# Query and key projections of an attention stage as 512- and 256-column products into two PSUM banks each

## The reference

```python
for i in range(DEPTH):
    x = x + 0.5 * swiglu(rmsnorm(x, ln_gains[i, 0]), w_gate[i, 0], w_up[i, 0], w_down[i, 0])
    h = rmsnorm(x, ln_gains[i, 1])
    x = x + (moba_attention(h, w_qkv, w_o) if i % 2 == 0 else pool_mixer(h, pool_w, pool_scale))
    x = x + 0.5 * swiglu(rmsnorm(x, ln_gains[i, 2]), w_gate[i, 1], w_up[i, 1], w_down[i, 1])
return rmsnorm(x, final_gain)
```

## Time and profile before

| | us |
|---|---|
| median of 3 runs | 876.4 (876.39 to 876.97) |
| profiled execution | 878.0, of which the span from first to last instruction is 876.0 |
| TensorE busy | 866.6 |
| VectorE busy | 642.9 |
| ScalarE busy | 463.2 |
| weight loads on TensorE (beside its products) | 763.4 |

### The profile page before, as it was taken

One profiled execution on the slowest core, in us unless ns is written; L12 is line 12 of the kernel. 1 busy time (PEld: TensorE's weight loads), 2 busy tenths in 40 slices (PEclk: granted clock), 3 DMA queues, 4 the chain that ended last, 5 costly groups with the idle time before them and its releaser, 6 DMA issues.

```text
span 876.0 us, 12479 instructions
## 1 busy us (share of the span) xinstructions
PE 866.6 (99%) x5234; PEld 763.4 (87%) x5234; DVE 642.9 (73%) x742; ACT 463.2 (53%) x536; POOL 22.7 (3%) x49
## 2 busy tenths in 40 slices
PE   8999999999999999999999999999999999999997
PEld 7888888889999988888888888888888988888886
DVE  6998776568776699777656697777656998777452
ACT  6665555345555666555534375555544675555441
POOL 1000005300000000000000000000000000000000
PEclk9999999999999999999999999999999999999999
DMA  8677555565434447555455556555565277565431
GB/s 285 197 249 231 191 176 174 181 201 180 149 144 146 144 137 247 193 191 182 164 196 187 185 187 200 191 192 181 170 196 175 97 241 234 184 213 186 146 119 48
DMA packets 154166, 159.68 MB, mean 182 GB/s; under 512 B 2888, under 2 KB 152448, under 8 KB 154112
## 3 DMA queue, kind: packets, MB, share of 16 engines
q1 hardware_dynamic: 153760, 158.35, 55.5%
q10 hardware_dynamic: 352, 0.55, 0.2%
HBM read 157.84 MB, written 1.05 MB: 181 GB/s over the span
## 4 chain that ended last, share of the span: by engine, by line
PE 98%; DMA 1%; DVE 0%; SPq 0%; ACT 0%; issue 0%; DVEq 0%; ACTq 0%
PE psum L430 97%; DMA band<-in_x_dram 1%; PE psum L744 1%; PE psum L727 1%; PE psum L460 0%; PE psum L618 0%; ACT soft L917 0%; SPq L366 0%; SPq L364 0%; DVE band L1184 0%; DVE scratch L1227 0%; DVE scratch L1196 0%; DVEq L75 0%; DVE mean L1208 0%; DVE rstd L1091 0%
## 5 line engine op out<-in xcount | busy, mean ns | idle before, releaser
L430 PE MATMUL psum<-xg,w_hi 128*128 128x512 f32 (+1 forms) x1664 | 490.1, 379 | 0.1
L1046 DVE TENSOR_TENSOR w_lo<-raw,w_hi 128x2048 fp32r<-128x2048 f32 (+1 forms) x149 | 332.3, 2232 | 109.8 <-ACT w_hi L825 109.8
L430 PEld LDWEIGHTS psum<-xg,w_lo 128*128 128x128 f32 x1536 | 289.0, 188 | 62.5
L825 ACT ACTIVATE w_hi<-raw 128x2048 fp32r<-128x2048 f32 (+1 forms) x150 | 279.5, 1867 | 112.5 <-PE psum L430 112.0
L430 PE MATMUL psum<-xg,w_lo 128*128 128x256 f32 x1536 | 312.8, 278 | 0.0
L430 PEld LDWEIGHTS psum<-xg,w_hi 128*128 128x128 f32 x1664 | 254.4, 189 | 1.8 <-issue 0.9
L430 PE MATMUL psum<-h_all,w_hi 128*128 128x512 f32 (+1 forms) x656 | 189.4, 374 | 0.0
L430 PEld LDWEIGHTS psum<-h_all,w_lo 128*128 128x128 f32 x592 | 111.4, 188 | 23.4
L430 PE MATMUL psum<-h_all,w_lo 128*128 128x256 f32 x592 | 121.8, 278 | 0.0
L430 PEld LDWEIGHTS psum<-h_all,w_hi 128*128 128x128 f32 x656 | 100.2, 189 | 0.8 <-issue 0.8
L859 ACT ACTIVATE scratch<-psum 128x512 f32<-128x512 f32 x44 | 26.1, 594 | 80.8 <-PE psum L430 80.8
(11 more groups left out here) (114 smaller groups left out, 477.5 us busy)
## 6 DMA issues: line engine op xcount, KB each, us to landing
raw<-in_ffn_w_up_dram SPq DMA_DIRECT2D x43, 1024.0 KB, 5.1
raw<-in_ffn_w_gate_dram SPq DMA_DIRECT2D x42, 1024.0 KB, 5.1
raw<-in_ffn_w_down_dram SPq DMA_DIRECT2D x24, 1024.0 KB, 5.2
raw<-in_attn_w_qkv_dram SPq DMA_DIRECT2D x12, 1024.0 KB, 5.2
raw<-in_ffn_w_down_dram SPq DMA_DIRECT2D x20, 512.0 KB, 4.4
raw<-in_ffn_w_down_dram SPq DMA_DIRECT2D x12, 768.0 KB, 4.4
raw<-in_attn_w_o_dram SPq DMA_DIRECT2D x4, 1024.0 KB, 4.9
band<-in_x_dram SPq DMA_DIRECT2D x4, 256.0 KB, 5.2
```

The source lines that it names most:

```text
L430: return nc.tensor.matmul(out, stationary, moving, start=start, stop=stop, skip_group_check=True)
L825: nc.scalar.activation(w_hi[:, n % SPL, 0:size], raw[:, n % RAW, 0:size], ACT.Copy).then_inc(hi_split, 1)
L1046: nc.vector.tensor_tensor(w_lo[:, n % SPL, 0:size], raw[:, n % RAW, 0:size], w_hi[:, n % SPL, 0:size].bitcast(f32), ALU.subtract).then_inc ...
```

## The change

Q and K tiles use `split_products`: per chunk and column half one 512-column product and one 256-column product. Each column half m has a bank of its own, so Q takes banks 0 and 1, K banks 2 and 3, and V moves to bank 0. The scores of quads 0 to 2 move to banks 4 to 7, the output of quads 0 to 2 to bank 3. ScalarE copies the correction halves of Q and K into `q_sb` and `k_sb` (`copy_corrections`); VectorE adds the main halves, waits for that addition, and scales in place.

The waits on TensorE change with the banks. The Q tile of quad j waits for `qkv_scaled >= 3 * j`, the V scaling of the quad before, where it waited for the Q scaling of that quad. The K tile of quads 2 and 3 waits for the output of quad j - 2. The V tile waits for the Q scaling of its own quad, and did not wait at all for quad 0. `values(j, 0)` waits for the K scaling of quad j + 1. The first output tile waits for `o_lo` of quad 0 alone. The orders in which VectorE and ScalarE call their steps stay as they were, with `copy_corrections` put in.

```diff
         def head_bank(quad, hh):
-            return (3, 4, 5, 6)[hh] if quad < QUADS - 1 else (3, 1, 0, 2)[hh]
+            return (4, 5, 6, 7)[hh] if quad < QUADS - 1 else (1, 2, 0, 3)[hh]
         def o_bank(quad):
-            return (7, 7, 0, 3)[quad]
+            return 3 if quad < QUADS - 1 else 1
+        def qk_acc(s):
+            return psum[:, 2 * s:2 * s + 2, :]
...
-                    for m in range(GM):
-                        cols = slice(m * P, (m + 1) * P)
-                        last = passes(acc_bank(b)[:, m, :], hi[:, k, cols], lo[:, k, cols], xg_hi[:, k, :],
-                                      xg_lo[:, k, :], start=(k == 0 and m == 0), stop=(k == DC - 1))
+                    last = split_products([(banks[m], hi[:, k, m * P:(m + 1) * P], lo[:, k, m * P:(m + 1) * P],
+                                            xg[:, k], k == 0, k == DC - 1) for m in range(GM)])
...
-                if j:
-                    pe.wait_ge(qkv_scaled, 3 * (j - 1) + s + 1)
-                elif s == 0:
-                    pe.wait_ge(x_done, DC + 6)
+                if s == 0:
+                    if j:
+                        pe.wait_ge(qkv_scaled, 3 * j)
+                    else:
+                        pe.wait_ge(x_done, DC + 6)
+                elif s == 1:
+                    if j > 1:
+                        pe.wait_ge(o_lo_done, j - 1)
+                else:
+                    pe.wait_ge(qkv_scaled, 3 * j + 1)
                 if s < 2:
-                    column_product(n, s, norm, stats_norm)
+                    column_product(n, (2 * s, 2 * s + 1), norm, stats_norm)
                     return
...
-                        out = psum[:, 2, t * GW:(t + 1) * GW]
+                        out = psum[:, 0, t * GW:(t + 1) * GW]
...
-                pe.wait_ge(o_lo_done, max(j + 1, 2))
+                pe.wait_ge(o_lo_done, j + 1)
...
-                    if j == QUADS - 2:
-                        pe.wait_ge(qkv_scaled, 3 * (QUADS - 1) + 1)
+                    if j < QUADS - 1:
+                        pe.wait_ge(qkv_scaled, 3 * (j + 1) + 2)
...
+            def copy_corrections(j, s):
+                act.wait_ge(tile_used, ATT0 + 3 * j + s + 1)
+                nc.scalar.activation((q_sb, k_sb)[s][:, j % 2], qk_acc(s)[:, :, SEQ:2 * SEQ],
+                                     ACT.Copy).then_inc(qk_corr, 1)
+            copy_corrections(0, 0)
+            copy_corrections(0, 1)
             split_hi(ATT0 + SPL)
             split_hi(ATT0 + 1 + SPL)
...
-                    split_hi(ATT0 + 3 * j + 2 + SPL)
-                    split_hi(ATT0 + 3 * j + 3 + SPL)
+                    for s in range(2):
+                        split_hi(ATT0 + 3 * j + 2 + s + SPL)
+                        copy_corrections(j + 1, s)
...
             def qkv_scale(j, s):
-                dve.wait_ge(tile_used, ATT0 + 3 * j + s + 1)
+                if s < 2:
+                    done = 2 * j + s + 1
+                    qk = (q_sb, k_sb)[s][:, j % 2]
+                    dve.wait_ge(qk_corr, done)
+                    nc.vector.tensor_tensor(qk, qk_acc(s)[:, :, 0:SEQ], qk, ALU.add).then_inc(qk_sum, 1)
+                    dve.wait_ge(qk_sum, done)
                 if s == 0:
-                    ins = nc.vector.scalar_tensor_tensor(out=q_sb[:, j % 2], in0=acc_bank(0), scalar=HD ** -0.5,
-                                                         in1=rstd_m, op0=ALU.mult, op1=ALU.mult)
+                    ins = nc.vector.scalar_tensor_tensor(out=qk, in0=qk, scalar=HD ** -0.5, in1=rstd_m,
+                                                         op0=ALU.mult, op1=ALU.mult)
                 elif s == 1:
-                    ins = nc.vector.tensor_tensor(k_sb[:, j % 2], acc_bank(1), rstd_m, ALU.mult)
-                else:
+                    ins = nc.vector.tensor_tensor(qk, qk, rstd_m, ALU.mult)
+                else:
+                    dve.wait_ge(tile_used, ATT0 + 3 * j + s + 1)
                     for t in range(TT):
-                        ins = nc.vector.tensor_scalar(v_sb[:, j % 2, t, :], psum[:, 2, t * GW:(t + 1) * GW],
+                        ins = nc.vector.tensor_scalar(v_sb[:, j % 2, t, :], psum[:, 0, t * GW:(t + 1) * GW],
```

More of the change, by code:

```diff
@@ L208, in build_trunk @@
         qkv_scaled = sem("qkv_scaled")
+        qk_corr = sem("qk_corr")
+        qk_sum = sem("qk_sum")
         score_done = sem("score_done")
@@ L639, in _, with column_product @@
             ffn(0)
-            def column_product(n, b, norm=None, stats_norm=None):
+            def column_product(n, banks, norm=None, stats_norm=None):
                 hi, lo = col_tile(w_hi, n), col_tile(w_lo, n)
```

## The result

The changed kernel takes 890.3 us (median of 5, 887.8 to 891.6) against 877.0 us before: a ratio of 1.0148 (1.0137 to 1.0158), 13.4 us slower. A second set of runs gave 889.3 and 877.1, ratio 1.0132 (1.0119 to 1.0146), 12.2 us slower. The forecast was 887.3, 10.9 us slower, in a range of 885.5 to 890.5; of the 3.0 us between forecast and median 0.6 lies in the base, which was 876.4 when the forecast was made. The measured median is 0.2 us inside the upper end of the range.

A forecast was written before the change was run, and what follows sets the result against it. TensorE, busy 99% of the span, was taken as the bound, so every new wait adds in full. -1.48 (products) + 2.87 and 7.95 (stalls) + 1.6 (clock) = +10.9 us on 876.4: 887.3 us, range 885.5 to 890.5.

The forecast's parts named there:

- Part 1: Query and key tiles: one 512- and one 256-column product a group gain 0.185 us a tile, 1.48 us in all.
- Part 2: Correction copies on ScalarE (4.8 us) and additions on VectorE (some 5.7 us) cost nothing while under TensorE's stream.
- Part 3: V of quad 0, now sharing bank 0, must wait for Q's scaling: TensorE stalls 2.9 us.
- the short stall: TensorE's wait ahead of V of quad 0 for Q of quad 0 to be scaled, put at 2.9 us.
- Part 4: Q of quad 1 waits for V of quad 0, scaled behind the softmax work: TensorE stalls 7.95 us.
- the long stall: TensorE's wait ahead of Q of quad 1 for V of quad 0 to be scaled, put at 7.95 us.
- Part 5: Other new waits in the steady loop cause no stall; the thinnest, V's for Q's scaling, has 0.4 us to spare.
- the cover: Time to spare between Q's scaling and the next quad's V tile: 0.4 us in quad 1, larger in quad 0.
- Part 6: After the 7.95 us without work TensorE's clock may fall to 1.2 GHz: 1.6 us lost, bounds 0 to 3.2.
- that rival: The clock falls in the 2.9 us stall ahead of V of quad 0 too: another 1.6 us, 888.9; 9%.
- the start's stretch: Program start taken to run at half rate until between 3.6 and 4.93 us; 3.5 us at half rate sized the clock loss.

The follow-up runs named there:

- V first: The changed kernel, but VectorE scales V of quad 0 ahead of the softmax of quad 0, not behind it; 879.8 us, ratio 1.0024.
- V between the parts: Against V first in its own bank: VectorE scales V of quad 0 between the two lower weight parts ahead of the softmax; 877.9 us, ratio 1.0008.
- the long fill alone: The changed kernel with 32 idle 512-column products on TensorE ahead of the wait before Q of quad 1; 888.1 us.
- both fills: The changed kernel with idle 512-column products ahead of both waits: 11 before V of quad 0, 32 before Q of quad 1; 886.7 us.
- the short fill: The 11 idle products ahead of V of quad 0, added to the long fill alone to make both fills; 886.7 us with it.
- V first in its own bank: Against V first: V of quad 0 goes to bank 7, and the second half of its scores waits for V's scaling; 879.6 us.

## Why the prediction was right, and where it was off

*Part 1, the products.* Right in kind: 0.17 us a tile measured by the loop's period, not 0.185, so 1.3 to 1.4 us in all.

*Part 2, the additions and copies.* Right within 0.2 us: with all of them in place, no stalls and products as wide as before, the stage takes 74.96 us against 74.76.

*Part 3, the short stall.* 2.9 us expected, 2.81 measured. The chain was the one described; VectorE in the changed kernel:

```profile
206.08 0.43 DVE L1111 SCALAR_TENSOR_TENSOR rstd<-rms_sq,rstd 128x258 f32<-128x258 f32 x1
206.55 0.69 DVE L1332 TENSOR_TENSOR scratch<-psum,scratch 128x512 f32<-128x512 f32 x1
207.27 0.69 DVE L1335 SCALAR_TENSOR_TENSOR scratch<-scratch,rstd 128x512 f32<-128x512 f32 x1
```

*Part 4, the long stall.* 7.95 us expected, 8.00 measured. From the first bias to V's scaling takes 7.59 us, against 7.60 before:

```profile
215.00 0.55 DVE L1351 SCALAR_TENSOR_TENSOR score<-dist,psum 128x384 f32<-128x384 f32 x1 [1.31 <-PE psum L436]
...
222.59 0.87 DVE L1342 TENSOR_SCALAR v_sb<-psum,rstd 128x256 f32<-128x256 f32 x2
```

Moving that one call took the stall away, so VectorE's order is its cause, shown and not only argued.

*Part 5, the steady loop.* Right: no stall in quads 1 and 2, and the cover was as thin as said. In the changed kernel Q of quad 2 is scaled at 258.00 + 0.69 = 258.69, and its V tile starts at 259.00:

```profile
258.00 0.69 DVE L1335 SCALAR_TENSOR_TENSOR scratch<-scratch,rstd 128x512 f32<-128x512 f32 x1
...
259.00 0.36 PE L436 MATMUL psum<-w_hi,xg 128*128 128x256 f32 x1
```

In quad 0 a stall lets VectorE get ahead of TensorE, as said, but it need not be the long one: with V first, where only the short stall is left, V of quad 1 doesn't wait either. With both stalls gone and a weight part ahead of the softmax the cover failed by 1.0 us, in the kernel with V between the parts.

*Part 6, the clock.* This is the term that was mis-sized. For the long stall of the profiled execution it is right: the products right behind it run at 1.2 GHz, and three pairs of groups take 227.33 - 223.60 = 3.73 us, where the same three, right behind the scores too, take 2.22 with V first: a loss of 1.5 us against the 1.6 expected.

```profile
223.60 1.19 PE L436 MATMUL psum<-xg,w_hi 128*128 128x512 f32 x2 [8.00 <-DVE v_sb L1342]
...
225.02 1.05 PE L436 MATMUL psum<-xg,w_hi 128*128 128x512 f32 x2
...
227.33 0.63 PE L436 MATMUL psum<-xg,w_hi 128*128 128x512 f32 x2
228.03 0.63 PE L436 MATMUL psum<-xg,w_hi 128*128 128x512 f32 x2
```

That it came so close is partly luck. The prediction took its size from the start of the program and checked it by the mean clock of 0.998, whose 1.75 us of lost clock it laid to the start. The row of the kernel before's last 6 us shows where that loss is recorded:

```profile
870.00:876.00 6.00, 0.00 (x0) 0.00 (x0) 2.58 (x11) 1.83 (x6) 0.00 (x0) 0.68 0.45 171
```

A clock of 0.68 over 6 us is 1.9 us, with TensorE idle, so it costs nothing; the rows of the first 8 us read 1.00, although eight transposes take 1.97 us there and twelve of the attention stage 1.47. So the mean clock does not bear out the start's stretch, and the timeline of the transposes was the only evidence.

What was missing is the short stall, which costs a stretch of its own in some runs. The prediction gave that rival 9% and a price of 1.6 us. In the second profiled execution of the changed kernel it happened: the stage took 1.2 us more than in the first. With the long fill alone it happened too, and with both fills the stage is 86.17 - 84.60 = 1.6 us shorter. The price was fair and the chance too low, since two of four profiled executions with this wait show it. By medians the short fill takes off 888.1 - 886.7 = 1.3 us, but those are four runs each on two chips, and their ratios to before differ by 0.0007 only, or 0.6 us, so this can't size it.

The sum with what was measured: 877.0 - 1.3 (products) + 10.8 (idling) + 0.3 (left over) = 886.8 without any loss of clock, where both fills give 886.7. With 1.5 for the long stall it is 888.3, and with 1.2 to 1.6 more, in the executions in which the short stall costs too, 889.5 to 889.9; the second set ran from 887.9 to 890.3. The first set's slowest, 891.2 and 891.6 at a clock of 0.989, lie above that. A stretch as dear as the one of 2.9 us behind the 2.6 us wait (V first in its own bank) would give 888.3 + 2.9 = 891.2. No profile of such a run is there, so this is an estimate, and what made those runs slow stays open.

## What to carry to other kernels

When accumulators move to other banks, the waits move too: for each new one ask at what place in the other engine's program its signal is given, and what stands ahead of it there, since the signal of a short operation behind a long block comes when the block does. A change worth 1.3 us on TensorE brought two waits worth 10.8, and moving one call gave back 9.5. Price a stall on TensorE as its idle time, 0.1 to 0.2 us beyond it, and a slow stretch after it: 1.5 us behind the stalls of 4 and 8 us here, and in some executions 1.2 to 2.9 us even behind one of 2.6 to 2.8 us. Where the start blurs the run times, compare one stage in the traces.

## What the runs showed of the hardware

A stall of 2.6 to 2.8 us was followed by 1.2 GHz in some executions and not in others: granted clock of 0.83 over 206 to 216 us in one of the changed kernel, 1.00 in another, with the same wait of 2.81 us. No slow stretch followed the waits of 1.0 and 0.4 us in the profiled execution of the kernel that has them (mean clock 1.000); its other ten runs read 0.998 or 0.999, which can't exclude one. Idling for 4.0 us and for 8.0 us cost the same beyond the idle time, 1.5 to 1.6 us in the traces, and the dearest stretch, some 2.9 us, came behind 2.62 us. The clock recorded at the end of the program falls while TensorE is idle there (0.68 over the last 6 us before), which moves the mean clock of a run by up to 0.002 at no cost. The start of the program varies by about 1.5 us between executions and sets the limit of what medians can tell here: 11 runs a kernel left +- 0.5 us on a difference that the loop's period gives to a few hundredths.
